# Token rows of the last two experts handed over by 0/1 matrix products, the other rows gathered earlier

## The chip, the cores and the metric

One core of one Trainium2 chip. The time is device microseconds (us) of one execution of the program; what counts is the median over runs.

## What is computed

One step of a one-layer decoder on 512 prompt tokens and 8 x 4 sample tokens (544 rows of 1024 values). After the mixer half (mLSTM memory, causal pooling, projections, layer norm) comes the part that matters here, a mixture of 16 experts with two chosen for each token, and the last layer norm:

```
vals, idx = lax.top_k(jnp.where(in_group, probs, -1.0), TOP_K)      # TOP_K = 2 of 16 experts
wts = vals / jnp.sum(vals, -1, keepdims=True)
gate = jnp.sum(jax.nn.one_hot(idx, N_EXPERTS) * wts[..., None], axis=1)
h = silu(einsum('nd,edf->nef', xt, w_e_gate)) * einsum('nd,edf->nef', xt, w_e_up)
h = h * gate[..., None]
moe = einsum('nef,efd->nd', h, w_e_down)
x = _layer_norm(ALPHA * x + moe, ln2_g, ln2_b)
```

## The kernel before

Every engine has its own program, written by hand in five functions (`_(sp)`, `_(pl)`, `_(ac)`, `_(ve_)`, `_(pe)`), and waits on semaphores by count. There is no scheduler: each engine runs its list in order, so what stands behind a waiting instruction waits too.

Tokens are held in `NT` = 5 row tiles (four of 128 rows and one of 32). For each expert up to `CAP` = 96 tokens have a slot. POOL gathers their rows from the DRAM copy `x1_rows` (`gather`, L739), PE transposes them (`rows_in`, L2146), `up` (L2159) makes gate and up products in PSUM banks 2 and 3, ACT and DVE make the hidden rows (`gate_sigmoid` L1055, `silu` L1643), `hidden_in` (L2179) and ACT (L1051) turn them, and `down` (L2173) makes the 96 result rows in PSUM banks 4 and 5. ACT and DVE copy them to `ys` (L1059; L1649, L1651), and POOL stores them in the DRAM array `y_slots` (`store_y`, L745). The weights of the experts alternate between two sets of buffers that SP fills. One `turn` on PE is: up(e), rows_in(e+1), down(e-1), hidden_in(e).

After the last turn only `down` of expert 15 is left; it waits until ACT and DVE have copied expert 14's result out of the same banks (L2233, L2234). Expert 15's rows are stored by SP in two halves (L664, L666).

The tail gives the tokens their two expert rows. `gather_rows(0, ...)` (L784) fetches, for each row tile, the row of each token's lower-numbered expert (`ya`); it waits for the store of expert 14. `gather_rows(1, ...)` fetches the row of the other expert (`ybk`); it waits for the two halves of expert 15 (`last_out`). Then for each tile: DVE x1 = ya * gate + x1 (L1715); PE adds x1 by an identity (`sum_start`, L2267) and ybk by a diagonal of gates (`sum_end`, L2274) into PSUM; DVE takes the statistics (`stats`, L1723 to L1726) and centres (`centred`, L1730); POOL makes the inverse root (L798); ACT scales (L1113); POOL adds the tile to the output in DRAM (L808), where SP has put the bias before. SP waits for all of them at the end.

Each engine also carries a block `if extra > 0` for experts with more than 96 tokens: it loads a number from `ctl` and branches. It stands between the turns and the tail, and is not entered with these inputs.

## Time and profile before

| | |
|---|---|
| median of 3 runs | 899.44 us (898.88 to 900.25) |
| the profiled execution | 900.57 us, its span 899.3 us |
| PE busy | 867.6 us, 96% of the span |
| DVE, ACT, POOL busy | 360.5, 206.3, 85.6 us |
| mean granted TensorE clock | 0.990 of full speed |
| share of PE in the chain that ended last | 91% |
| idle time of PE before the tail's first product | 5.35 us |
| span after the last product of expert 15 | 37.5 us |

The span runs from the first to the last instruction. PE is busy nearly everywhere except in the last 40 us, where the work is a chain over DMA, PE and DVE.

### The profile page before, as it was taken

Reading aid. Unit: us, or ns where it says so; the run is one execution under the profiler, and the core shown is the slowest. Engines: PE = TensorE matmul, PEld = TensorE weight load, DVE = VectorE, ACT = ScalarE, POOL = GpSimd, SP = SyncE. Lnnn points to the kernel's source line nnn. Section 1 sums busy time; section 2 is a strip of 40 time slices with the busy share of each in tenths; the row PEclk is TensorE's granted clock in tenths of the full one; section 3 lists DMA queues with packets and bytes.
Section 4 is the critical chain, followed back from the end, with each engine's and each line's share of the span. In section 5 each row is a group of like instructions: output and inputs, shape, how many; then the busy total and the mean of one; then the engine's idle time right before and its main releaser. Section 6 shows DMA issues by size and latency. Waiting matters only on the chain.

```text
span 899.3 us, 20975 instructions
## 1 busy us (share of the span) xinstructions
PE 867.6 (96%) x9437; PEld 710.4 (79%) x9437; DVE 360.5 (40%) x749; ACT 206.3 (23%) x313; POOL 85.6 (10%) x89
## 2 busy tenths in 40 slices
PE   7999999999999999999999999999999999999964
PEld 6999888898989999999999988666666566565631
DVE  5653645736575372233232555722311211111146
ACT  4521141311422332322221201231111111111112
POOL 1210000000000001001101021400001000100053
PEclk9999999999999999999999999999999999999987
DMA  9895171492816043222221923699999999999566
GB/s 323 268 286 152 48 264 65 146 313 64 280 48 211 1 156 93 84 67 87 94 95 47 378 102 151 243 371 400 401 404 405 398 410 411 406 404 424 215 210 125
DMA packets 85374, 203.47 MB, mean 226 GB/s; under 512 B 4237, under 2 KB 57189, under 8 KB 76472
## 3 DMA queue, kind: packets, MB, share of 16 engines
q1 hardware_dynamic: 78216, 177.17, 53.5%
q0 software_dynamic: 7088, 25.26, 9.1%
q8 instruction: 57, 0.93, 0.4%
q14 instruction: 13, 0.11, 0.0%
HBM read 172.58 MB, written 32.06 MB: 228 GB/s over the span
## 4 chain that ended last, share of the span: by engine, by line
PE 91%; DMA 4%; DVE 2%; ACT 1%; issue 1%; POOL 0%; SPq 0%; DVEq 0%; POOLq 0%
PE psum L2159 18%; PE psum L465 17%; PE psum L467 17%; PE psum L466 16%; PE psum L2173 9%; PE psum L1863 2%; DMA xg<-x_rows,idx_i 2%; PE psum L1873 2%; PE psum L2146 2%; PE psum L1902 1%; PE psum L2105 1%; PE psum L2072 1%; DMA ya_rows<-y_slots,dest_i 1%; DMA xn<-in_x_prompt_dram 1%; PE psum L1888 1%; PE psum L2037 1%
## 5 line engine op out<-in xcount | busy, mean ns | idle before, releaser
L465 PE MATMUL psum<-x_hi,split_lo 128*128 128x272 f32 x704 | 208.9, 297 | 2.0 <-DVE pbl L1427 1.2
L467 PE MATMUL psum<-x_hi,split_hi 128*128 128x272 f32 x704 | 202.3, 287 | 0.0
L466 PE MATMUL psum<-x_lo,split_hi 128*128 128x272 f32 x704 | 202.1, 287 | 0.0
L2159 PE MATMUL psum<-set,xt 128*32 128x256 f32 x3072 | 169.1, 380 | 0.0
L2159 PEld LDWEIGHTS psum<-set,xt 128*32 128x32 f32 x3072 | 98.2, 110 | 65.7 <-issue 2.4
L465 PEld LDWEIGHTS psum<-x_hi,split_lo 128*128 128x128 f32 x704 | 132.6, 188 | 7.3 <-issue 2.7
L466 PEld LDWEIGHTS psum<-x_lo,split_hi 128*128 128x128 f32 x704 | 132.8, 189 | 1.4 <-issue 1.0
L467 PEld LDWEIGHTS psum<-x_hi,split_hi 128*128 128x128 f32 x704 | 132.6, 188 | 0.0
L460 DVE TENSOR_TENSOR split_lo<-raw,split_hi 128x2048 fp32r<-128x2048 f32 x35 | 80.0, 2290 | 113.8 <-ACT split_hi L441 113.3
L2173 PE MATMUL psum<-set,hT 128*32 128x256 f32 x1536 | 86.2, 380 | 1.5 <-DVE ys L1651 1.5
L2173 PEld LDWEIGHTS psum<-set,hT 128*32 128x32 f32 x1536 | 49.0, 110 | 32.8 <-ACT hT L1051 1.7
L1643 DVE TENSOR_TENSOR gs<-psum,gs 128x384 f32<-128x384 f32 x16 | 8.9, 558 | 152.8 <-ACT gs L1055 152.8
L441 ACT CAST split_hi<-raw 128x2048 fp32r<-128x2048 f32 x35 | 66.7, 1907 | 1.3 <-DMA raw<-in_w_in_dram 1.2
L465 PE MATMUL psum<-split_hi,x_lo 128*128 128x256 f32 x160 | 46.6, 291 | 0.0
L467 PE MATMUL psum<-split_hi,x_hi 128*128 128x256 f32 x160 | 45.1, 282 | 0.0
L466 PE MATMUL psum<-split_lo,x_hi 128*128 128x256 f32 x160 | 44.9, 281 | 0.0
L1055 ACT ACTIVATE gs<-psum 128x384 f32<-128x384 f32 x16 | 7.9, 491 | 156.9 <-PE psum L2159 156.9
L467 PE MATMUL psum<-gh,split_hi 128*128 128x272 f32 x128 | 37.0, 289 | 0.0
L1649 DVE COPY ys<-psum 96x256 f32<-96x256 f32 x16 | 6.7, 421 | 75.4 <-PE psum L2173 75.4
L465 PE MATMUL psum<-gh,split_lo 128*128 128x272 f32 x128 | 36.8, 288 | 0.0
L466 PE MATMUL psum<-gl,split_hi 128*128 128x272 f32 x128 | 36.8, 287 | 0.0
L739 POOL DMA_INDIRECT xg<-x_rows,idx_i x16 | 22.9, 1433 | 143.9 <-PE psum L2146 129.3
(355 smaller groups left out, 1250.3 us busy)
## 6 DMA issues: line engine op xcount, KB each, us to landing
set<-in_w_e_gate_dram SPq DMA_DIRECT2D x32, 1024.0 KB, 18.3
set<-in_w_e_up_dram SPq DMA_DIRECT2D x32, 1024.0 KB, 20.9
set<-in_w_e_down_dram SPq DMA_DIRECT2D x32, 1024.0 KB, 21.2
raw<-in_w_in_dram SPq DMA_DIRECT2D x26, 1024.0 KB, 6.5
cb<-in_state_C_dram SPq DMA_DIRECT2D x8, 1024.0 KB, 7.9
out_dram<-cb SPq DMA_DIRECT2D x8, 1024.0 KB, 5.8
y_slots<-ys POOLq DMA_DIRECT2D x15, 384.0 KB, 7.3
y_slots<-x_hi POOLq DMA_DIRECT2D x3, 1536.0 KB, 14.8
```

The costliest lines, as they stand in the source:

```text
L441: nc.scalar.copy(split_hi[:, c % SPLIT_SLOTS, :], raw[:, c % RAW_SLOTS, :]).then_inc(w_hi, 1)
L460: nc.vector.tensor_tensor(split_lo[:, slot, :], raw[:, c % RAW_SLOTS, :], split_hi[:, slot, :].bitcast(F32), ALU.subtract).then_inc(w_lo, 1)
L465: nc.tensor.matmul(out, a_lo, b_hi, start=first, stop=False)
L466: nc.tensor.matmul(out, a_hi, b_lo, start=False, stop=False)
L467: return nc.tensor.matmul(out, a_hi, b_hi, start=False, stop=last)
L739: pl.indirect_dma_start(xg[e % 2][0:CAP], None, x1_rows, idx).then_inc(g_in[e % 2], 16)
L1863: last = mm(narrow(j)[:, 0:SEQ - i * P], kt[:, c, i * P:i * P + P], qt[:, c, i * P:SEQ], start=c == 0, stop=c == 1)
L1873: last = mm(narrow(j)[:, 0:VW], pb[:, at:at + P], ve[:, i, :], start=i == 0, stop=i == t)
L1888: last = mm(narrow(j)[g * NS:(g + 1) * NS, 0:VW], qm[:, c, 2 * g + b, :], cb[:, 2 * g + b, c, :], start=False, stop=q == 3)
L2146: last = nc.tensor.transpose(out[:, k // 4, k % 4], cols[:, k, :], ident[0:CAP, 0:CAP])
L2159: last = mm(gate_up()[32 * b:32 * b + 32, j], xt[:, kk, 32 * mine:32 * mine + 32], w, start=kk == 0 and j != 1, stop=kk == KT - 1 and j > 0)
L2173: last = mm(results()[32 * b:32 * b + 32, 256 * j:256 * j + 256], h_, w, start=kk == 0 and j != 1, stop=kk == QB and j > 0)
```

## The change

- **Order of the last experts.** PE does the first half of down(14), then turns the hidden rows of expert 15, then the second half, then down(15), whose result goes to PSUM banks 6 and 7 (`results_last`) and whose hidden rows go to an own buffer (`hT_last`), so it no longer waits for the copies of expert 14's result.
- **Rows of experts 14 and 15 stay on chip.** They aren't stored. SP writes zeros over their slots in `y_slots` early in the program (four DMAs of 192 KB), where POOL wrote one of 384 KB before. ACT and DVE multiply each of the 96 rows by its token's gate and split the product in two (`high_part`, `low_part`). Two 0/1 matrices, made by DVE once after turn 4 (`late_slots`), say which slot belongs to which token; PE multiplies them with both parts, straight into the sum (`add_late`).
- **The gates by slot** come from ten more small matrix products in `rows_of(5)` and five more DVE steps in `choice_gates`.
- **Gathers** now wait for the store of expert 13 (and, for the second ones, for up(14)).
- **The second expert's rows** are scaled by ACT (`scaled_second`) and added by POOL (`add_second`) for the four large tiles, in place of PE's diagonal products; for the small tile DVE does it.
- **The block for overfull experts** stands behind the tail on every engine (and makes the output anew if it is entered).

```diff
@@ SP
+                for e in (NE - 2, NE - 1):
+                    for c in (0, 512):
+                        sp.dma_start(y_slots[e * CAP:(e + 1) * CAP, c:c + 512], const("head_sel")[32:32 + CAP, 0:512]
+                                     ).then_inc(zero_out, 16)
...
-        sp.wait_ge(ya_ok, NE)
-        sp.dma_start(y_slots[(NE - 1) * CAP:NE * CAP, 0:512], ys[1][0:CAP, 0:512]).then_inc(last_out, 16)
-        sp.wait_ge(yd_ok, NE)
-        sp.dma_start(y_slots[(NE - 1) * CAP:NE * CAP, 512:DM], ys[1][0:CAP, 512:DM]).then_inc(last_out, 16)
+        sp.wait_ge(outs, 16 * NT)
+        sp.wait_ge(cp_out, 16 * H)
         sp.wait_ge(xa_ok, 1)
         extra = sp.value_load(ctl[0:1, XTRA:XTRA + 1], min_val=0, max_val=XTRA)
@@ POOL
-        for e in range(NE - 4, NE - 1):
+        for e in range(NE - 4, NE - 2):
             store_y(e)
...
-        pl.wait_ge(ys_out[0], 16 * NE // 2)
+        pl.wait_ge(ys_out[0], 16 * (NE // 2 - 1))
         pl.wait_ge(ys_out[1], 16 * (NE // 2 - 1))
-        pl.wait_ge(dn_done, 2 * NE - 2)
         for i in range(NT):
             gather_rows(0, ya, i)
-        pl.wait_ge(last_out, 32)
+        pl.wait_ge(gu_done, 2 * NE - 2)
         for i in range(NT):
             gather_rows(1, yb_, i)
+        def add_second(i):
+            pl.wait_ge(xa2_ok, i + 1)
+            pl.wait_ge(act_rows, SCALED[i])
+            nc.gpsimd.tensor_tensor(x1[:, i, :], x1[:, i, :], yb_[i], ALU.add).then_inc(dg_ok, 1)
+        for i in range(PT):
+            add_second(i)
@@ ACT
+        def high_part(q, b):
+            at = slice(512 * b, 512 * b + 512)
+            ac.wait_ge(ya_ok, NE - 1 + q)
+            if b:
+                ac.wait_ge(yd_ok, NE - 1 + q)
+            nc.scalar.activation(late_y[q][0][0:CAP, at], ys[q][0:CAP, at], ACT.Copy, scale=gslot[0:CAP, q:q + 1]
+                                 ).then_inc(act_rows, 1)
+        def scaled_second(i):
+            ac.wait_ge(yb_in[i], 16)
+            nc.scalar.activation(yb_[i], yb_[i], ACT.Copy, scale=gates_ab[:, 1, i:i + 1]).then_inc(act_rows, 1)
+        gate_sigmoid(2 * NE)
+        ac.wait_ge(hi_done, NE)
+        nc.scalar.copy(hT_last[:], psum[:, 6, 0:QB * P].rearrange("p (q t) -> p q t", q=QB)).then_inc(ht_ok, 1)
+        ac.wait_ge(ys_out[0], 16 * (NE // 2 - 1))
+        store_half(0, 2 * NE - 2)
+        for b in range(2):
+            high_part(0, b)
+        for i in range(2):
+            scaled_second(i)
+        ac.wait_ge(ys_out[1], 16 * (NE // 2 - 1))
+        ac.wait_ge(dn_done, 2 * NE)
+        nc.scalar.copy(ys[1][0:CAP, 0:512], psum[0:CAP, 6, :]).then_inc(ya_ok, 1)
+        for b in range(2):
+            high_part(1, b)
+        for i in range(2, PT):
+            scaled_second(i)
@@ DVE
+        def low_part(q, b):
+            at = slice(512 * b, 512 * b + 512)
+            ve_.wait_ge(yd_ok, NE - 1 + q)
+            ve_.wait_ge(act_rows, HIGH[q][b])
+            v.scalar_tensor_tensor(late_y[q][1][0:CAP, at], ys[q][0:CAP, at], gslot[0:CAP, q:q + 1],
+                                   late_y[q][0][0:CAP, at].bitcast(F32), ALU.mult, ALU.subtract).then_inc(lo_y, 1)
@@ PE
+            if g == len(OH_FIRST) - 2:
+                for q in range(2):
+                    for i in range(NT):
+                        at = 96 * (3 + q)
+                        last = mm(psum[0:CAP, 7, at:at + 96].rearrange("p (a q) -> p a q", a=32), onehot[:, i, NE - 2 + q, :],
+                                  gate3[:, i, q, :].unsqueeze(1).to_broadcast([P, 32, 3]), start=i == 0, stop=i == NT - 1)
...
+        down(0, 8 * NE, 0)
+        pe.wait_ge(hs_ok, NE)
+        hidden_in()
+        down(0, 8 * NE, 1)
         pe.wait_ge(ht_ok, NE)
-        pe.wait_ge(yd_ok, NE - 1)
-        pe.wait_ge(ya_ok, NE - 1)
         for half in range(2):
-            down(1, 8 * NE, half)
+            down(1, 8 * NE, half, hT_last, results_last)
+        def own_rows(i, first=True):
+            r = ROWS[i]
+            pe.wait_ge(xa2_ok, i + 1 if i < PT else NT + 1)
+            pe.wait_ge(dg_ok, min(i + 1, PT))
+            if i >= PT:
+                pe.wait_ge(pf_ok, i - PT + 1)
+            for b in range(2):
+                mm(summed(i)[0:r, b, :], ident[0:r, 0:r], x1[0:r, i, b * 512:b * 512 + 512], start=first, stop=False)
+        def add_late(i, q, first=False):
+            r = ROWS[i]
+            pe.wait_ge(act_rows, HIGH[q][1])
+            pe.wait_ge(lo_y, 2 * q + 2)
+            for part in (1, 0):
+                for b in range(2):
+                    last = mm(summed(i)[0:r, b, :], late[q][0:CAP, P * i:P * i + r],
+                              late_y[q][part][0:CAP, b * 512:b * 512 + 512], start=first and part == 1, stop=q == 1 and part == 0)
+            if q:
+                last.then_inc(pc_ok, 1)
```

How the instructions stand, in two places. On PE, from down(14) on, before (`set_133` and `set_134` are the two weight sets, `x_130` is x1):

```order
L2173 MATMUL psum<-set_133,hT 32x256 x48
L2179 MATMUL psum<-cst,hs 128x128 x3
L2173 MATMUL psum<-set_134,hT 32x256 x48
...
L2267 MATMUL psum<-x_130,cst 128x512 x6
L2274 MATMUL psum<-ybk,diag 128x512 x2
L2267 MATMUL psum<-x_130,cst 128x512 x2
L2274 MATMUL psum<-ybk,diag 128x512 x6
```

and now, up to the end of the second tile (`oh_160` and `oh_194` are the 0/1 matrices of experts 14 and 15):

```order
L2306 MATMUL psum<-set_133,hT 32x256 x24
L2312 MATMUL psum<-cst,hs 128x128 x3
L2306 MATMUL psum<-set_133,hT 32x256 x24
L2306 MATMUL psum<-set_134,hT_last 32x256 x48
L2393 MATMUL psum<-y_lo,oh_160 128x512 x2
L2393 MATMUL psum<-y_hi,oh_160 128x512 x2
...
L2385 MATMUL psum<-x_130,cst 128x512 x2
L2393 MATMUL psum<-y_lo,oh_194 128x512 x2
L2393 MATMUL psum<-y_hi,oh_194 128x512 x2
```

The turning of expert 15's hidden rows moved into the middle of down(14), and each tile's pair of diagonal products gave way to eight with the 0/1 matrices, those of expert 14 ahead of the first two tiles' own rows. On DVE, between the last `silu` and the first statistics, now:

```order
L1713 TENSOR_TENSOR hs<-psum,gs 128x384
L1774 SCALAR_TENSOR_TENSOR x_130<-ya_rows,gates_ab,x_130 128x1024 x2
L1718 COPY ys_172<-psum 96x256
L1720 COPY ys_172<-psum 32x256 x3
L1774 SCALAR_TENSOR_TENSOR x_130<-ya_rows,gates_ab,x_130 128x1024
L1781 SCALAR_TENSOR_TENSOR y_lo<-ys_172,gslot,y_hi 96x512 x2
L1774 SCALAR_TENSOR_TENSOR x_130<-ya_rows,gates_ab,x_130 128x1024
L1795 COPY ys_173<-psum 96x256
L1797 COPY ys_173<-psum 32x256 x3
L1781 SCALAR_TENSOR_TENSOR y_lo<-ys_173,gslot,y_hi 96x512 x2
L1774 SCALAR_TENSOR_TENSOR x_130<-ya_last,gates_ab,x_130 32x1024
L1804 SCALAR_TENSOR_TENSOR x_130<-ybk,gates_ab,x_130 32x1024
```

where before the four copies of expert 14 and the four of expert 15 were followed by the five additions of ya. The first two additions now stand ahead of the copy of expert 14's result.

## Rows read from the trace of the kernel before

**Rows 1.** Chain of waits of the last 100 us: start us, us, what

```profile
838.33 0.48 PE psum L2179 x3
...
849.31 5.22 PE psum L2173 x96
...
863.41 8.18 DMA ya_rows<-y_slots,dest_i
```

**Rows 2.** Timeline of the tail: start us, us, engine, line, instruction [idle before <-releaser]

```profile
856.47 5.39 PE L2173 MATMUL psum<-set,hT 128*32 128x256 f32 x96 [1.50 <-DVE ys L1651]
...
860.82 1.03 POOL L784 DMA_INDIRECT ya_rows<-y_slots,dest_i  x1 [3.19 <-DMA y_slots<-ys]
862.15 0.95 POOL L784 DMA_INDIRECT ya_rows<-y_slots,dest_i  x1 [0.30 <-issue]
862.22 0.42 DVE L1649 COPY ys<-psum 96x256 f32<-96x256 f32 x1 [5.85 <-PE psum L2173]
862.65 1.31 DVE L1651 COPY ys<-psum 32x256 f32<-32x256 f32 x3
...
865.77 1.28 DVE L1715 SCALAR_TENSOR_TENSOR x<-ya_rows,gates_ab,x 128x1024 f32<-128x1024 f32 x1 [1.81 <-DMA ya_rows<-y_slots,dest_i]
...
867.20 7.81 PE L2267 MATMUL psum<-x,cst 128*128 128x512 f32 x12 [5.35 <-issue]
...
876.84 1.30 DVE L1723 BATCH_NORM_STATS2 lst<-psum 128x6 f32<-128x512 f32 x2 [1.45 <-PE psum L2274]
...
885.86 1.28 DVE L1723 BATCH_NORM_STATS2 lst<-psum 128x6 f32<-128x512 f32 x2
...
888.68 1.27 DVE L1723 BATCH_NORM_STATS2 lst<-psum 32x6 f32<-32x512 f32 x2
```

**Rows 3.** Granted clock by stretch: us, POOL busy, clock, DMA share, GB/s

```profile
864.00:865.00 1.00, 0.70 (x2) 0.80 0.85 320
...
871.00:872.00 1.00, 0.90 (x1) 0.79 0.66 111
```

**Rows 4.** The store of expert 13: timeline row, and its issue (KB each, us to landing)

```profile
840.70 0.51 POOL L745 DMA_DIRECT2D y_slots<-ys  x1 [16.82 <-DVE ys L1651]
...
y_slots<-ys POOLq DMA_DIRECT2D x1, 384.0 KB, 5.6
```

**Rows 5.** Timeline, PE: split-type products of 272 columns; full products of 512 columns

```profile
199.83 0.19 PEld L465 LDWEIGHTS psum<-x_hi,split_lo 128*128 128x128 f32 x1
...
200.81 0.19 PEld L467 LDWEIGHTS psum<-x_hi,split_hi 128*128 128x128 f32 x1
...
878.28 5.31 PE L2274 MATMUL psum<-ybk,diag 128*128 128x512 f32 x12
```

**Rows 6.** By line on POOL: duration ns min/median/max, first and last start

```profile
L724 POOL TENSOR_TENSOR sg<-sg,yb x8: 1360/1360/2195, 353.3 to 482.9; 128x544 f32<-128x544 f32 x8
...
L728 POOL TENSOR_TENSOR hrs<-hve,cst x5: 1509/1517/1527, 517.2 to 555.4; 128x1 f32<-128x1 f32 x4, 32x1 f32<-32x1 f32 x1
...
L798 POOL TENSOR_TENSOR hrs<-hve,cst x5: 549/555/563, 878.7 to 890.5; 128x1 f32<-128x1 f32 x4, 32x1 f32<-32x1 f32 x1
```

**Rows 7.** Timeline of two places where DVE and POOL meet

```profile
352.01 2.29 DVE L460 TENSOR_TENSOR split_lo<-raw,split_hi 128x2048 fp32r<-128x2048 f32 x1 [7.81 <-ACT split_hi L441]
...
353.33 2.19 POOL L724 TENSOR_TENSOR sg<-sg,yb 128x544 f32<-128x544 f32 x1 [85.08 <-ACT yb L999]
...
572.94 7.45 DVE L1572 TENSOR_TENSOR onehot<-cst,tmp_r 128x288 bf16<-128x288 f32 x20
...
573.29 7.93 POOL L739 DMA_INDIRECT xg<-x_rows,idx_i  x1 [1.22 <-DVE idx_i L1587]
```

**Rows 8.** Timeline, PE: the 15 small products of one `rows_of`

```profile
646.98 0.82 PEld L2130 LDWEIGHTS psum<-tok_bf,onehot 128*96 128x96 bf16 x15
```

**Rows 9.** Timeline of SP behind its branch

```profile
865.47 0.93 SPq L679 DMA_DIRECT2D out_dram<-nrows  x2
```

**Rows 10.** Timeline of DVE: the silu of expert 5, where the matrices come before it

```profile
676.36 0.56 DVE L1643 TENSOR_TENSOR gs<-psum,gs 128x384 f32<-128x384 f32 x1 [9.69 <-ACT gs L1055]
```

More of the change, by code:

```diff
@@ L297, in build @@
     yb_ = [ybk[:, i, :] for i in range(NT)]
+    hT_last = place("hT_last", [P, QB, P], F32, r_ht + NT * DM * 4)
+    oh15 = place("oh15", [P, N], F32R, at_route + DM * 4)
+    late = (oh14, oh15)
+    y14_hi, y14_lo = lay(r_ht + (NT * DM + QB * P) * 4, r_ht + 4 * CHUNK * 4,
+                         ("y14_hi", [P, DM], F32R), ("y14_lo", [P, DM], F32R))
+    y15_hi, y15_lo = lay(r_moe, end, ("y15_hi", [P, DM], F32R), ("y15_lo", [P, DM], F32R))
+    late_y = ((y14_hi, y14_lo), (y15_hi, y15_lo))
     psum = ctx.enter_context(nc.psum_tensor("psum", [P, 8, 512], F32))
@@ L1655, in _, with late_slots @@
         choice_gates()
+        def late_slots():
+            found = psum[0:CAP, 7, 3 * 96:5 * 96].rearrange("p (e c) -> p e c", c=96)[:, :, 0:3]
+            step(v.tensor_reduce(gslot[0:CAP], found, AX.X, ALU.add))
+            step(v.tensor_copy(tok_f[0:CAP], idx_i[0:CAP, NE - 2:NE]))
+            for i in range(NT):
+                last = v.tensor_scalar(tok_at[0:CAP, :, i:i + 1].rearrange("p e o -> p (e o)"), tok_f[0:CAP],
+                                       float(1 - P * i), None, ALU.add)
+            step(last)
+            for q, oh in enumerate(late):
+                for i in range(NT):
+                    r = ROWS[i]
+                    last = v.tensor_scalar(oh[0:CAP, P * i:P * i + r], const("slot", CAP)[:, 0:r], tok_at[0:CAP, q, i:i + 1],
+                                           None, ALU.is_equal)
+            step(last)
         def turn(e, odd, y_used=None):
@@ L1672, in _ @@
         turn(4, False, y_used=(ys_out[1], 16))
+        ve_.wait_ge(idx_ok, 6)
+        late_slots()
         with ve_.Fori(2, NE // 2 - 1) as t:
@@ new lines, in low_part @@
+        def low_part(q, b):
[4 more added lines that the diff above has]
+                                   late_y[q][0][0:CAP, at].bitcast(F32), ALU.mult, ALU.subtract).then_inc(lo_y, 1)
+        silu(NE - 1)
+        for i in range(2):
+            add_first(i)
+        ve_.wait_ge(ys_out[0], 16 * (NE // 2 - 1))
@@ new lines, in _ @@
+        store_half(0, 2 * NE - 2)
+        add_first(2)
+        low_part(0, 0)
+        low_part(0, 1)
+        add_first(3)
+        ve_.wait_ge(ys_out[1], 16 * (NE // 2 - 1))
+        ve_.wait_ge(dn_done, 2 * NE)
+        v.tensor_copy(ys[1][0:CAP, 512:768], psum[0:CAP, 7, 0:256])
+        for b in range(QB):
+            last = v.tensor_copy(ys[1][b * 32:b * 32 + 32, 768:DM], results_last()[CAP:P, 256 * b:256 * b + 256])
+        last.then_inc(yd_ok, 1)
+        low_part(1, 0)
+        low_part(1, 1)
@@ L1681, in _, with centred @@
+        def centred(i):
+            r = ROWS[i]
+            v.scalar_tensor_tensor(x1[0:r, i, :], summed(i)[0:r].rearrange("p b n -> p (b n)"), hmv[0:r, i, 0:1],
+                                   lng[0:r, :], ALU.subtract, ALU.mult).then_inc(pf_ok, 1)
+        stats(0)
+        for i in range(NT):
+            centred(i)
+            if i < NT - 1:
+                stats(i + 1)
         extra = ve_.value_load(ctl[0:1, XTRA:XTRA + 1], min_val=0, max_val=XTRA)
@@ L2161, in up, with down @@
             last.then_inc(gu_done, 1)
-        def down(p, loaded, half):
+        def down(p, loaded, half, hT=hT, results=results):
             pe.wait_ge(set_in[p][4 + half], loaded)
```

206 lines of the change are left out of this document (114 added, 92 removed).

## The prediction, made before the changed kernel ran

> **What bounds the kernel now.** I read the page first: PE is busy 96% of the span, so up to the last expert only PE's own work counts. Then the chain of waits of the last 100 us, which stays on PE up to down(14), from 849.31 to 854.53 [rows 1], and then leaves it. The timeline shows the rest: down(15) from 856.47 to 861.83 [rows 2]; the store of expert 14, after which POOL may issue the first gather at 860.82; the gathers of ya, of which one took 8.18 us from issue to landing [rows 1]; PE idle for 5.35 us until its first identity product at 867.20 [rows 2]; and from 876.84 on DVE, whose tiles follow each other every 888.68 - 885.86 = 2.82 us, up to the fifth at 888.68 [rows 2]. From there to the end of the span is 899.3 - 888.68 = 10.62 us (statistics, scaling, the last addition to DRAM). The change touches this tail of some 45 us, and elsewhere almost nothing. The reader should see one thing: DVE's statistics start 15 us after down(15) has ended, and those 15 us are what can be won.
>
> **The working, in the times of the trace before.**
>
> *Last down.* With the turning of expert 15's hidden rows (0.48 us [rows 1]) inside down(14), which alone ends at 854.53, PE is through with both by 855.0, and down(15) follows at once: 855.0 + 5.36 = 860.4 instead of 861.83, 1.4 us sooner.
>
> *Gathers.* The store of expert 13 is issued at 840.70 and lands after 5.6 us [rows 4], at 846.3. The first gather then starts at 846.6, after the same 0.27 us as now, 14.2 us sooner than 860.82. Each costs POOL 0.95 us and a gap of 0.30 [rows 2], ten of them 12.5 us, to 859.1. Landing takes between 4.95 us (ya of tile 0: 860.82 to the addition at 865.77 [rows 2]) and 8.18 [rows 1]; I take 5, because the weights, the two stores of SP and the store of expert 14 no longer run beside them. So ya is in DVE's hands from 851.6 on, and the last ybk lands near 864.
>
> *DVE's queue.* Behind silu(15): two additions of ya (1.28 us each [rows 2]), the copies of expert 14 (0.42 + 1.31 [rows 2], from 855.1), one addition, two low parts, one addition, which ends at 860.9; the copies of expert 15 to 862.65; two low parts, the addition and the product of the small tile. A low part of 96x512 isn't in the trace; between the 0.42 us of a copy of 256 columns and the 1.28 us of 1024 columns [rows 2] I take 0.72. With nothing in its way DVE is ready for statistics at 866.7.
>
> *POOL's additions* are new: four of 128x1024. The nearest row is 1.36 us for 544 columns [rows 6]; without a fixed part that gives 2.56 us, with the 0.55 us of the tiny ones [rows 6] as fixed part 2.07. I take 2.4. The GPSIMD Engine Reference of the Trainium skill, Performance versus the Vector engine, has 4.497 us for 2048 columns, of which half would be 2.25; the sum would move by under a microsecond.
>
> *PE's sums.* An identity pair (full precision) costs what the diagonal one did: four records at 0.43, 1.72 us a tile (12 records in 5.31 [rows 5]). A 0/1 product takes the split type. 272 columns follow each other every (200.81 - 199.83) / 8 = 0.1225 us [rows 5]; 512 columns cost 0.22 by columns. Its dearer bound is the full-precision product, 0.86. I take 0.22, as type and shape of the nearer row are the same. A tile from the third on costs 1.72 + 8 x 0.22 = 3.5 us, more than DVE's 2.82, so PE becomes the slower of the two there by 0.7 us a tile.
>
> *Who shares with whom.* This decides the sum. An addition on POOL beside a DVE instruction with both tensors in SBUF took 2.19 us instead of 1.36: it started at 353.33 and DVE ended at 354.30 [rows 7]. A gather issued beside 7.45 us of such DVE work took 7.93 us [rows 7]. The inverse roots of line 728, which meet line 1516 (x1 and ln gain, both SBUF), took 1.52 us; those of line 798, which meet line 1730 (PSUM and gain), 0.55 [rows 6]. So POOL stands still until DVE is done. Whether DVE stands still for POOL no row shows: no DVE row is stretched. By the SBUF page of the Trainium skill, SBUF: two separate sides, the pair of ports is an exclusive lock and "the other fully blocks", either way. The rows on POOL's side agree with it; a gain from an addition that runs free of DVE would need it not to hold.
>
> With blocking: POOL's gathers end near 860.5. The first addition waits for DVE's fourth (860.9) and runs to 863.3, and DVE's low part, due at 862.7, waits for it. Then DVE's four instructions, all ready, run without a gap (2 x 0.72 + 2 x 1.28 = 4.0 us) to 867.3, as the twenty in rows 7 did, and POOL's three remaining additions follow: 869.7, 872.1, 874.5. PE: own rows and both experts of tile 1 end at 872.3, tile 2 at 875.8, tile 3 at 879.3, tile 4 at 882.8. DVE waits for each. The fifth statistics start at 882.9 instead of 888.68; the span would end at 893.5.
>
> *The clock.* PE then pauses from 866.0 to 869.7. Before, the granted clock went to 0.5 between 864 and 865, about 2.8 us into the pause that began at 861.83, and came back after 871, 4.2 us after PE resumed [rows 3]. A pause of 3.7 us may do the same; 4.2 us at half speed cost 2.1 us. I count half, 1.0.
>
> *Small terms.* Ten more small products in `rows_of(5)`: 15 take 0.82 us, so 10 x 0.055 = +0.55 on PE, in full, since PE is the bound there [rows 8]. The 17 DVE steps of `late_slots` fit in the 9.69 us DVE idles before the silu of expert 5 [rows 10], even at its 0.56 us each (9.5); without this cover what exceeds would delay PE's hidden rows. The five steps in `choice_gates` have a similar gap and cost nothing. The zeroing on SP (four issues, 0.77 MB) goes among weight loads three buffers ahead: nothing; uncovered, under 2 us. The overflow block now runs on SP behind the last landing: SP issued the next DMA at 865.47 [rows 9], at most 1.5 us after DVE's copies had let it go on (862.65 + 1.31 [rows 2]), with the issue of a store inside that. Between 0 and 1.5 I take +0.8. On the other engines it hides behind the 6 us in which the last output lands.
>
> Sum: 893.5 + 1.0 + 0.55 + 0.8 = 895.85 for the span against 899.3, a gain of 3.45 us. The profiled execution had 900.57 us, so 897.1 for such a one; against the median of 899.44, **896.0 us**. What a measurement can tell from no change is about 0.2%, 1.8 us.
>
> **The rivals.**
>
> *Turns alternate.* If POOL gets in between any two DVE instructions, each POOL addition delays one of DVE's four. DVE then ends at about 862.7 + 4.0 + 3.3 x 2.4 = 874.6, its tiles follow at 2.82 us, the fifth at 885.9, the span ends at 896.5, and 897.9 with the small terms: 1.4 us less, **898.0 us**. For it: the block as a rule applies both ways. Against: rows 7, where POOL got in only at the end of DVE's run. 25%.
>
> *No blocking.* Additions run beside DVE: statistics from 866.8, PE's 3.5 us tiles end at 878.4, the span at 889.1, 890.4 with the small terms, 8.9 us less: **890.5 us**. Against: rows 6 and 7. It stays possible in part, if the meetings fall elsewhere. 20%.
>
> *Slower: the clock stays low.* PE has 32 split products and five identity pairs after 863, 7.1 + 8.6 = 15.7 us at full clock. If the broken pattern (wait for POOL, 1.7 to 3.5 us of work, wait) keeps the clock at half, they take 31.4 us at least less what hides in waits: from 863.3 to about 890.4, the span ends at 901.0, 902.4 with the small terms, 3.1 us more: **902.5 us**. It decides if the granted clock is 0.5 beyond 875. For it: before, half clock held from 865 to 871 over a busy PE [rows 3]. Against: it came back during just such work. 11%.
>
> *It doesn't do what it says*: gathers landing so late that nothing is won, within 0.2% of 899.4. With 8.2 us to land, the first two additions hold up expert 14's copies by 2 us and little is left of the gain. 4%.
>
> **How the numbers follow.** The forecast has 40%, the rivals 25, 20, 11 and 4. The range 889.6 to 899.9 reaches from below the free case over the alternating one with 2 us of late landing; it leaves out the low clock and some edges. Faster by over 0.2% (below 897.6): the forecast but for its edge (36), no blocking (20), a fifth of the alternating case (5): 0.61. Slower: the low clock, 0.11. Within: 0.28.
>
> **What would show it.** Right: the first gather near 847.2; down(15) without idle before it; no PE idle of 5 us; POOL's additions 2.4 us each or longer where they meet DVE's additions and low parts; PE waiting for POOL's additions from the second tile on; 0/1 products 0.22 us apart; one short stretch at clock 0.5 near 870. Wrong: DVE instructions of 1.28 us stretched to over 2 (alternating), POOL's additions finished by 871 (free), PE at 0.5 beyond 875 (low clock), or 0/1 products 0.4 us apart at full clock, which would put some 6 us on PE and bring back the old time.

## The result, and the profile after

The changed kernel takes **902.21 us** (median, 898.18 to 904.56), the kernel before 899.46 us on the same chip (898.32 to 900.79): a ratio of 1.0027, 95% interval 1.0014 to 1.0039, so 2.4 us slower by the ratio. The prediction said 896.0 us, faster by more than 0.2% with a chance of 0.61, and a range up to 899.9. It was wrong in sign and outside its range. The times of the changed kernel also scatter over 6.4 us, those of before over 2.5 in these twelve runs and over 3.5 to 4.9 in the larger sets beside the experiments.

The profiled execution had 901.96 us, its span 900.7 us. Timeline of the tail (start us, us, engine, line, instruction [idle before <-releaser]), against [rows 2]:

```profile
842.50 0.51 POOL L762 DMA_DIRECT2D y_slots<-ys  x1 [16.82 <-DVE ys L1720]
849.38 1.01 POOL L785 DMA_INDIRECT ya_rows<-y_slots,dest_i  x1 [6.38 <-DMA y_slots<-ys]
...
862.63 0.87 POOL L785 DMA_INDIRECT ybk<-y_slots,dest_i  x1 [0.30 <-issue]
...
863.53 9.27 POOL L798 TENSOR_TENSOR x<-x,ybk 128x1024 f32<-128x1024 f32 x4
...
865.99 8.02 DVE L1781 SCALAR_TENSOR_TENSOR y_lo<-ys,gslot,y_hi 96x512 fp32r<-96x512 f32 x2 [1.50 <-ACT y_hi L1140]
...
866.04 2.38 PE L2385 MATMUL psum<-x,cst 128*128 128x512 f32 x4 [1.90 <-POOL x L798]
866.41 2.17 ACT L1145 ACTIVATE ybk<-ybk,gates_ab 128x1024 f32<-128x1024 f32 x2
...
874.16 1.19 PE L2393 MATMUL psum<-y_lo,oh 96*128 96x512 f32 x2 [5.74 <-DVE y_lo L1781]
...
876.55 1.30 DVE L1812 BATCH_NORM_STATS2 lst<-psum 128x6 f32<-128x512 f32 x2
...
883.26 1.29 DVE L1812 BATCH_NORM_STATS2 lst<-psum 128x6 f32<-128x512 f32 x2 [0.66 <-PE psum L2393]
...
886.84 1.29 DVE L1812 BATCH_NORM_STATS2 lst<-psum 128x6 f32<-128x512 f32 x2 [0.66 <-PE psum L2393]
...
890.65 1.28 DVE L1812 BATCH_NORM_STATS2 lst<-psum 32x6 f32<-32x512 f32 x2 [0.89 <-PE psum L2393]
```

The pair of low parts of expert 15 took 8.02 us; the pair of expert 14, with the same shape, took 1.40. DVE was ready at 865.99, just after POOL had begun its second addition (at 865.85), and the pair ended at 874.03, after POOL's fourth (863.53 + 9.27 = 872.80). PE stood for 5.74 us behind it. The chain of waits says the same: here 6.24 us of "issue" are DVE standing in front of an instruction for which every semaphore was there. (That the landing of `ybk` stands ahead of it in the chain means nothing for the low part, which doesn't read these rows; the wait belongs to the product of the small tile behind it.)

```profile
862.63 4.36 DMA ybk<-y_slots,dest_i
866.99 0.03 issue
867.04 6.24 issue
873.28 0.75 DVE y_lo L1781
```

POOL itself was not slowed. By line, its durations (ns, min/median/max, first and last start):

```profile
L798 POOL TENSOR_TENSOR x<-x,ybk x4: 2330/2352/2369, 863.5 to 870.5; 128x1024 f32<-128x1024 f32 x4
```

The clock, against [rows 3] (stretch, us, busy PE, PEld, DVE, ACT, POOL, granted clock, DMA share, GB/s):

```profile
866.00:868.00 2.00, 1.96 (x4) 0.68 (x4) 2.00 (x1) 2.00 (x3) 2.00 (x1) 0.86 0.07 27
868.00:870.00 2.00, 0.42 (x1) 0.00 (x0) 2.00 (x1) 0.58 (x1) 2.00 (x2) 0.50 0.00 0
...
874.00:876.00 2.00, 1.84 (x4) 1.49 (x5) 1.97 (x3) 0.00 (x0) 0.00 (x0) 0.50 0.00 0
876.00:878.00 2.00, 2.00 (x4) 0.86 (x3) 1.94 (x4) 0.00 (x0) 0.00 (x0) 0.58 0.00 0
878.00:880.00 2.00, 2.00 (x8) 1.21 (x7) 1.74 (x4) 0.50 (x1) 0.57 (x1) 1.00 0.00 0
```

It fell to its lower level (1.2 GHz) between 867 and 868, while PE worked again behind a first idle of 1.90 us, so before the long pause; it stayed there through the pause and for the first 3.5 us of work after it. So the statistics start at 876.55, hardly sooner than the 876.84 of before [rows 2], and then follow at PE's pace of 3.57 us a tile instead of DVE's 2.82.

### The profile page after: what moved, and what is told of

Read it like the earlier page. It is cut to its first block, busy times and chain, and to the rows that moved or that the text cites. A ratio compares the mean times of both kernels' runs of the same rounds, so it can differ in the third digit from the quotient of the medians.

```text
span 900.7 us, 21087 instructions
## 1 busy us (share of the span) xinstructions
PE 870.3 (97%) x9467; PEld 714.9 (79%) x9467; DVE 374.8 (42%) x776; ACT 211.8 (24%) x316; POOL 93.4 (10%) x91
## 4 chain that ended last, share of the span: by engine, by line
PE 91%; DMA 3%; issue 2%; POOL 1%; DVE 1%; ACT 1%; DVEq 0%; SPq 0%; POOLq 0%
PE psum L480 17%; PE psum L482 17%; PE psum L481 16%; PE psum L2292 16%; PE psum L2306 8%; PE psum L1990 2%; DMA xg<-x_rows,idx_i 2%; PE psum L2000 2%; PE psum L2279 2%; PE psum L2029 1%; PE psum L2232 1%; PE psum L2199 1%; PE psum L2393 1%; PE psum L2385 1%; PE psum L2015 1%
## 5 line engine op out<-in xcount | busy, mean ns | idle before, releaser
L2306 PE MATMUL psum<-set,hT 128*32 128x256 f32 x1440 | 81.0, 380 | 0.0
L2306 PEld LDWEIGHTS psum<-set,hT 128*32 128x32 f32 x1440 | 45.3, 110 | 29.8 <-issue 0.2
L480 PEld LDWEIGHTS psum<-split_hi,x_lo 128*128 128x128 f32 x160 | 30.2, 189 | 5.3 <-issue 5.3
```

The source lines that it names most:

```text
L480: nc.tensor.matmul(out, a_lo, b_hi, start=first, stop=False)
L2306: last = mm(results()[32 * b:32 * b + 32, 256 * j:256 * j + 256], h_, w, start=kk == 0 and j != 1, stop=kk == QB and j > 0)
```

## The experiments

The theory after the result: POOL's unbroken run of four additions keeps DVE's low part out of SBUF, and PE, the clock and the whole tail follow. The rivals: PE's longer tiles are the bound in any case; the gathers are late; the low clock is the loss; the new order of the last experts doesn't gain.

**One wait: three of the additions behind the low parts.**

```diff
         for i in range(PT):
+            if i == 1:
+                pl.wait_ge(lo_y, 4)
             add_second(i)
```

> The changed kernel with one wait more: POOL does only its first addition when it is ready, the other three wait until DVE has made all four low parts. Theory (POOL's unbroken run of four additions keeps DVE's low part out): the pair of low parts starts near 866 and takes 1.4 us instead of 8.02, PE has no pause of 5.7 us, the granted clock stays at 1.0 after 866, the additions 2 to 4 take their turn after DVE's two products of the small tile (870), and the fifth statistics start near 886 instead of 890.65: some 4.5 us less than the change, about 897.5 us. Rival (the low part is slow for another reason, such as ACT writing its operand or the data): the pair still takes about 8 us and the time stays at 902. Rival (POOL's total of 9.3 us is the bound, whoever goes first): the additions end near 877 and PE's 3.57 us tiles behind them bring the fifth statistics to 890 to 891, no gain.

Measured: 897.20 us (895.11 to 899.24), ratio to before 0.9974 (0.9961 to 0.9988). One added wait takes some 5 us off the change. Timeline:

```profile
865.96 1.41 DVE L1783 SCALAR_TENSOR_TENSOR y_lo<-ys,gslot,y_hi 96x512 fp32r<-96x512 f32 x2 [1.86 <-ACT y_hi L1142]
...
867.45 8.93 POOL L798 TENSOR_TENSOR x<-x,ybk 128x1024 f32<-128x1024 f32 x3 [1.95 <-DVE y_lo L1783]
868.59 3.24 DVE L1806 SCALAR_TENSOR_TENSOR x<-ybk,gates_ab,x 32x1024 f32<-32x1024 f32 x1
...
886.45 1.28 DVE L1814 BATCH_NORM_STATS2 lst<-psum 32x6 f32<-32x512 f32 x2 [0.89 <-PE psum L2395]
```

The pair takes 1.41 us, the fifth statistics come at 886.45 (expected 886). One thing was not expected: DVE's second small product, issued at 868.59, got in after one addition (3.24 us), and POOL's additions, 3.3 us each twice, waited for DVE in turn. The clock still fell, to 0.50 in 872 to 874, after a later pause of PE (2.24 us, for the second addition), where it had been expected to stay at 1.0.

**No POOL additions: DVE adds the second rows.**

```diff
+        def second(i):
+            ve_.wait_ge(xa2_ok, i + 1)
+            ve_.wait_ge(yb_in[i], 16)
+            v.scalar_tensor_tensor(x1[:, i, :], yb_[i], gates_ab[:, 1, i:i + 1], x1[:, i, :], ALU.mult, ALU.add).then_inc(dg_ok, 1)
...
+        second(0)
         low_part(1, 0)
         low_part(1, 1)
+        for i in range(1, PT):
+            second(i)
```

> The changed kernel with the rows of the second expert added by DVE (product and addition in one instruction of 1.28 us, the first tile's before the low parts, the rest behind them) instead of ACT's scaling and POOL's addition. Theory (POOL's additions are what costs): low parts 0.7 us each, no pause of PE over 2 us, no half clock after 866, the statistics of tile 0 start near 875 (DVE's queue is 4 x 1.28 us longer) and follow every 3.57 us at PE's pace or 2.82 at DVE's, since PE is ahead by then; the fifth near 886.5, total 897 to 898.5 us. Rival (PE's tiles of 3.57 us are the bound wherever they start): the fifth statistics at 890 and 901 to 902 us. Rival (the late gathers are the bound): the second tile's rows land after 870 and DVE waits for a DMA in the tail.

Measured: 895.41 us (894.43 to 896.46, seven runs), ratio 0.9954 (0.9937 to 0.9971), with a scatter of 2 us instead of 6.

```profile
865.16 1.41 DVE L1780 SCALAR_TENSOR_TENSOR y_lo<-ys,gslot,y_hi 96x512 fp32r<-96x512 f32 x2
...
872.68 1.29 DVE L1814 BATCH_NORM_STATS2 lst<-psum 128x6 f32<-128x512 f32 x2
...
883.99 1.27 DVE L1814 BATCH_NORM_STATS2 lst<-psum 32x6 f32<-32x512 f32 x2
```

DVE has 5.1 us more to do and the fifth statistics come 6.7 us sooner. They follow every 2.83 us, so PE's tiles of 3.57 us, started early enough, are no bound, and DVE waits for no landing after 863.96; both rivals fall. Two details were missed: the time is 1.6 us below the expected range (the first statistics come at 872.68 instead of 875), and the clock was at half in 866 to 868. The version also takes four scalings off ACT, so it is less clean a test than the added wait.

**One operand moved: what kind of DVE instruction is kept out.**

```diff
+            src = psum[0:CAP, 6, :] if (q, b) == (1, 0) else ys[q][0:CAP, at]
-            v.scalar_tensor_tensor(late_y[q][1][0:CAP, at], ys[q][0:CAP, at], gslot...
+            v.scalar_tensor_tensor(late_y[q][1][0:CAP, at], src, gslot...
```

> The changed kernel with one operand moved: the first low part of expert 15 takes its result rows from PSUM instead of the copy in SBUF; all else is as in the change. Theory (what a POOL addition keeps out is a DVE instruction with two tensors in SBUF): this low part runs at 866 in 0.7 us beside POOL's additions; the second, which still has both in SBUF, waits until POOL has ended near 873, so the total stays within 1 us of the change (902). Rival (POOL keeps out any DVE instruction that touches SBUF, or ACT's write of the high part is what the low part waits for): the first stays stretched to 7 us or starts late.

Measured: 901.48 us (895.70 to 903.12), ratio 1.0013 (0.9996 to 1.0030).

```profile
862.77 9.26 POOL L798 TENSOR_TENSOR x<-x,ybk 128x1024 f32<-128x1024 f32 x4
...
865.22 0.75 DVE L1782 SCALAR_TENSOR_TENSOR y_lo<-psum,gslot,y_hi 96x512 fp32r<-96x512 f32 x1 [1.49 <-ACT y_hi L1140]
...
865.88 6.71 DVE L1782 SCALAR_TENSOR_TENSOR y_lo<-ys,gslot,y_hi 96x512 fp32r<-96x512 f32 x1
```

Two instructions, one behind the other, of the same shape and writing to the same kind of buffer: with one tensor from PSUM 0.75 us in the middle of POOL's run, with both in SBUF 6.71 us, to the run's end. So it is the second SBUF operand that lets POOL hold DVE up; the time of the whole doesn't move, since the second low part still waits. The SBUF page of the Trainium skill ("SBUF — State Buffer", Who interferes with whom) has the same border: a DVE instruction with two SBUF inputs contends, one with a single SBUF input doesn't. The trace agrees.

**PE kept busy in the pause.**

```diff
             own_rows(i, False)
+            if i == 0:
+                for _ in range(26):
+                    mm(psum[:, 4, :], late[0][0:CAP, 0:P], late_y[0][0][0:CAP, 0:512], start=True, stop=True)
             add_late(i, 1)
```

> The changed kernel with 26 additional products of 512 columns (split type, result not used) on PE in the place where it waits for the low parts of expert 15, so that TensorE does not pause. Theory (the pause costs twice, by itself and by the half clock after it): POOL and DVE as in the change; the granted clock stays at 1.0 from 868 to 878, the first two tiles' products go at full clock, 1.5 to 2 us are won: 900.3 us. Rival (the low clock is the main loss): over 4 us won, below 898. Rival (clock without effect, since the first tile hides it): within 0.5 us of the change, 902.

Measured: 901.09 us (897.95 to 904.49), ratio 1.0012 (0.9995 to 1.0029).

```profile
864.87 8.15 DVE L1781 SCALAR_TENSOR_TENSOR y_lo<-ys,gslot,y_hi 96x512 fp32r<-96x512 f32 x2 [1.46 <-ACT y_hi L1140]
...
866.55 8.02 PE L2404 MATMUL psum<-y_hi,oh 96*128 96x512 f32 x26
...
889.14 1.28 DVE L1812 BATCH_NORM_STATS2 lst<-psum 32x6 f32<-32x512 f32 x2 [0.88 <-PE psum L2393]
```

The clock was at 1.00 from 870 on. The filling ran at half clock at first (an earlier pause of 2.14 us had lowered it) and ended at 874.57, 1.6 us after the low parts, and gave part of the gain back. From its end to the fifth statistics are 14.57 us; in the change, from the end of the low parts, 890.65 - 874.03 = 16.62 us. The half clock costs 2.0 us in these two executions. By the ratios about 1.3 us are won, but the two intervals overlap, so the gain of the whole is not clear of noise; a gain of over 4 us, the first rival, is excluded.

**The new order of the last experts alone**, in the kernel before:

```diff
-        turn(NE - 1, True, 8 * NE, 8 * NE, None)
...
+        down(0, 8 * NE, 0)
+        pe.wait_ge(hs_ok, NE)
+        hidden_in()
+        down(0, 8 * NE, 1)
+        pe.wait_ge(ht_ok, NE)
+        for half in range(2):
+            down(1, 8 * NE, half, hT_last, results_last)
```

> The kernel before with the new order of the last experts alone: the first half of down(14), the turning of expert 15's hidden rows, the second half, and down(15) with its own buffer and its result in banks 6 and 7. By the prediction's term: down(15) starts 1.4 us sooner and all behind it with it, 899.2 - 1.4 = 897.8 us. Rival (the gathers of ya are the bound, since they wait for the store of expert 14, whose copies come no sooner): DVE's first addition stays at 865.8, and the time within 0.5 us of the kernel before.

Measured: 899.55 us (898.77 to 903.54), ratio 1.0012 (1.0001 to 1.0024): no gain.

```profile
855.31 5.36 PE L2188 MATMUL psum<-set,hT_last 128*32 128x256 f32 x96
...
857.92 0.51 POOL L751 DMA_DIRECT2D y_slots<-ys  x1 [16.34 <-DVE ys L1662]
...
861.41 1.02 POOL L790 DMA_INDIRECT ya_rows<-y_slots,dest_i  x1 [2.78 <-DMA y_slots<-ys]
...
866.30 1.28 DVE L1730 SCALAR_TENSOR_TENSOR x<-ya_rows,gates_ab,x 128x1024 f32<-128x1024 f32 x1 [3.75 <-DMA ya_rows<-y_slots,dest_i]
```

down(15) starts 1.2 us sooner than in [rows 2], but down(14), with the turning inside it, ends later, so the store of expert 14 leaves at 857.92 instead of 856.92 (0.4 us of it because the whole tail started later in this execution), and the gathers wait for that store. DVE's first addition comes at 866.30, no sooner than before, so the rival holds. In the change the gathers no longer wait for this store and down(14), the turning and down(15) together are 1.6 us shorter on PE (from 12.73 to 11.16 us); what that is worth to the time of the whole there was not tested.

**A semaphore between the additions.**

```diff
+            if i:
+                pl.wait_ge(dg_ok, i)
             nc.gpsimd.tensor_tensor(x1[:, i, :], x1[:, i, :], yb_[i], ALU.add).then_inc(dg_ok, 1)
```

> The changed kernel with one wait more before each of POOL's additions but the first: for the semaphore of its own previous addition, so that the next is not ready at the moment the previous one ends. Theory (DVE is kept out because POOL's next addition is always ready): the gap lets DVE's first low part in at the next boundary, it takes 2.9 us or less instead of 7.3, the pause of PE falls from 5.7 to about 3 us, and the time to about 899.5. Rival (the gap is too short or does not count): the low part still waits for the fourth addition, 902.

Measured: 899.01 us (896.96 to 902.41), ratio to before 0.9997 (0.9985 to 1.0010).

```profile
864.26 3.50 DVE L1783 SCALAR_TENSOR_TENSOR y_lo<-ys,gslot,y_hi 96x512 fp32r<-96x512 f32 x2 [1.50 <-ACT y_hi L1142]
864.33 2.89 POOL L800 TENSOR_TENSOR x<-x,ybk 128x1024 f32<-128x1024 f32 x1 [0.17 <-POOL x L800]
867.39 2.60 POOL L800 TENSOR_TENSOR x<-x,ybk 128x1024 f32<-128x1024 f32 x1 [0.17 <-POOL x L800]
```

PE's pause for the low parts falls to 0.77 us, and a wait that the data don't need wins about 3 us over the change, by the ratios of twelve runs each. How the gap does it, this execution shows only in part: the first low part became ready at 864.26, just inside the gap (864.16 to 864.33), and so met no addition at all; the second got in at the next boundary, as it also did in faster executions without the added wait (below). The times still scatter over 5.5 us.

**The changed kernel again.**

> The changed kernel itself once more, for its scatter (898.2 to 904.6 us in twelve runs). Theory (the time hangs on when DVE's low part comes against POOL's run of additions, and on when the outputs land): the low part is kept out until the last addition has ended, in whatever run, and the pause of PE is 5 to 6 us; what differs between runs is the start of the tail and the landing of the last output. Rival (in the fast ones DVE gets in between two additions): the low part takes 2 to 5 us and the fifth statistics come 2 to 4 us sooner than at 890.65.

> The changed kernel once more, one look. In the profiled execution of 901.96 us DVE's low part waited until the fourth addition had ended (8.02 us for the pair), in that of 899.11 us it got in where POOL's third addition was not ready (4.75 us). Theory (this alone makes the scatter): a time near 899 goes with a pair of under 6 us, a time of 901 or more with one of 7 us or more. Rival: the time goes with the landing of the last output or the start of the tail instead.

The first of them had 899.11 us, the second 898.65:

```profile
862.01 4.70 POOL L798 TENSOR_TENSOR x<-x,ybk 128x1024 f32<-128x1024 f32 x2 [0.36 <-ACT ybk L1145]
...
865.25 4.75 DVE L1781 SCALAR_TENSOR_TENSOR y_lo<-ys,gslot,y_hi 96x512 fp32r<-96x512 f32 x2 [1.38 <-ACT y_hi L1140]
...
866.94 5.28 POOL L798 TENSOR_TENSOR x<-x,ybk 128x1024 f32<-128x1024 f32 x2 [0.24 <-ACT ybk L1145]
```

```profile
861.89 10.23 POOL L798 TENSOR_TENSOR x<-x,ybk 128x1024 f32<-128x1024 f32 x4 [0.41 <-ACT ybk L1145]
...
864.89 5.01 DVE L1781 SCALAR_TENSOR_TENSOR y_lo<-ys,gslot,y_hi 96x512 fp32r<-96x512 f32 x2 [1.18 <-ACT y_hi L1140]
```

In the first, POOL's third addition was not ready (ACT had not yet scaled its tile), and DVE slipped into the gap. In the second there was no such gap, and DVE got in all the same, after which the two engines took turns. Both fast times go with a pair of about 5 us, the time of 901.96 with one of 8.02, and the fifth statistics come at 887.55 and 887.43: the rival of the first expectation holds, DVE does get in between in the faster ones. But it is not this alone, as the theory of the second one had it: in both, the first gather was issued 1.0 us sooner (848.39 and 848.41 against 849.38). The fairest comparison is the execution with one operand in PSUM, whose first gather came at 848.57 and whose second low part was held: its fifth statistics came at 889.80, some 2 us later than in these two.

One thing differs in step with the outcome. In the three executions with a hold (the change, one operand in PSUM, PE kept busy) ACT had scaled tile 2, and POOL's third addition was ready, some 0.65 us before the second ended; in the two fast ones only 0.1 us after that end, and 0.15 us before it. The probes below show that this can't be the whole rule: there every addition was ready long before.

**The sharing by itself**: phases behind the end of the kernel, in which POOL makes a run of additions and DVE comes in at a chosen time (in the first three phases `bn_stats` from PSUM in front of DVE's products is its delay). Cut to its core:

```diff
@@ POOL
+        nc.gpsimd.tensor_tensor(held[:], minus_half[0:1, 0:1], minus_half[0:1, 0:1], ALU.add).then_inc(pr_p, 1)
+        for i in range(adds):
+            nc.gpsimd.tensor_tensor(ya_rows[:, i, :], yb_[0], yb_[1], ALU.add).then_inc(pr_p, 1)
@@ DVE
+            ve_.wait_ge(pr_p, PROBES_DONE[k] + 1)
+            v.bn_stats(lst[:, 0, 0, :], summed(0)[:, 0, :]).then_inc(pr_v, 1)
...
+            v.scalar_tensor_tensor(outs_[i][0:rows, 0:cols], yb_[2][0:rows, 0:cols], gates_ab[0:rows, 0, 0:1], yb_[3][0:rows, 0:cols],
+                                   ALU.mult, ALU.add).then_inc(pr_v, 1)
```

> The changed kernel with a piece behind its end that measures the sharing by itself (its results go into buffers that are no longer read; the time of the whole is of no interest). Five phases, each begun by both engines together. 1: POOL makes four additions of 128x1024 one behind the other, and 0.7 us after its start DVE comes with two products of 96x512, both tensors in SBUF. 2: the same with two products of 32x1024. 3: as 2, but DVE's second product waits for a semaphore of its first. 4: DVE comes first with four products of 128x1024 one behind the other, POOL with three additions. 5: as 4, but each product of DVE waits for a semaphore of the one before. Theory (whoever runs keeps the other out until its ready instructions are through): in 1, 2 and 3 DVE's first product takes 8 to 9 us, POOL's additions 2.3 each; in 4 POOL's first addition takes 5.1 + 2.3 = 7.4 us and DVE's products 1.28 each; in 5 the gap between DVE's products lets POOL in. Rival (it depends on the shape: products of 32 rows get in at the next boundary, those of 96 don't): 1 as above, in 2 and 3 DVE's first product takes about 3 us and POOL's second addition 3.3. Rival (turns always alternate, and the low parts waited for something else): in 1 too DVE's products take 2 to 3 us each.

```profile
898.20 10.12 POOL L862 TENSOR_TENSOR ya_rows<-ybk 128x1024 f32<-128x1024 f32 x4
...
899.08 2.00 DVE L1880 SCALAR_TENSOR_TENSOR y_lo<-ybk,gates_ab 96x512 fp32r<-96x512 f32 x1
901.01 2.82 DVE L1880 SCALAR_TENSOR_TENSOR y_hi<-ybk,gates_ab 96x512 fp32r<-96x512 f32 x1
...
931.54 8.89 POOL L862 TENSOR_TENSOR ya_rows<-ybk 128x1024 f32<-128x1024 f32 x3
931.72 3.24 DVE L1880 SCALAR_TENSOR_TENSOR y_lo<-ybk,gates_ab 128x1024 fp32r<-128x1024 f32 x1 [4.96 <-POOL held L860]
934.88 3.35 DVE L1880 SCALAR_TENSOR_TENSOR y_hi<-ybk,gates_ab 128x1024 fp32r<-128x1024 f32 x1
```

Turns alternated in all five phases, for every shape, with and without semaphores: this was the last rival, and it contradicts both the theory and what the change shows. One case was not made as planned: in the fourth and fifth phase POOL began 0.14 to 0.18 us before DVE, so a run of DVE that is under way when POOL's first addition comes stayed untested. The second probe varied what still differed (more `bn_stats` in front, `ya_rows[:, i, :]` or `yb_[0]` as POOL's first operand, waits, ACT):

> The changed kernel with seven phases behind its end, as in the probe before (results unused, total time of no interest). In each POOL makes four additions of 128x1024 and DVE comes with two products of 96x512. A: DVE comes 0.7 us after the start, in POOL's first addition (control). B: 2.8 us after it, in the second. C: as B, POOL's additions in place. D: as C, with two fulfilled semaphore waits before each. E: as B, with ACT writing 128x1024 all the while. F: as D, with ACT, and the real low parts. G: DVE comes 4.9 us after the start, in the third addition. In the first probe turns alternated, in the change they did not, so one of these differences must decide. Theory 1 (which addition DVE comes in): A alternates, B to F wait until POOL's fourth addition has ended, some 6.5 us. Theory 2 (ACT's traffic): E and F wait, the others alternate. Theory 3 (waits before POOL's additions, or in place): D and F, or C, D and F wait. Theory 4 (it is arbitration by chance): no pattern over the seven.

A, C, D and F alternated; B and E (7.1 us) and G (5.31 us) waited for the fourth addition. That spoke for "in place or not", which the third probe repeated:

> Nine more phases behind the end of the changed kernel, as in the second probe: POOL makes four additions of 128x1024, DVE comes with two products of 96x512. DVE comes 2.8 us after the start (in the second addition), or 4.9 us (in the third, phases 8 and 9). 1 and 3: POOL adds in place on one set of tiles; 2 and 4: into other tiles, as in phase B; 5: in place on x1, exactly the additions of the change; 6: as 5 with the real low parts; 7: as 6 with two fulfilled waits before each addition; 8: as 5, 9: as 1, DVE coming in the third. Theory (in place or not decides, as in the second probe): 2 and 4 wait for the fourth addition (7 us), all others alternate (2 to 3 us), which would leave the block in the change itself unexplained. Rival (who gets in at a boundary is fixed by nothing that these phases vary): the same form goes either way, 1 unlike 3, or 2 unlike 4, or 5 unlike 6.

Its phases 1, 3 and 8 (1 and 3 are the same code; the last line is the third addition of phase 8):

```profile
898.70 9.22 POOL L869 TENSOR_TENSOR ya_rows<-ya_rows,ybk 128x1024 f32<-128x1024 f32 x4
...
901.37 7.10 DVE L1908 SCALAR_TENSOR_TENSOR y_lo<-ybk,gates_ab 96x512 fp32r<-96x512 f32 x1
...
919.76 10.12 POOL L869 TENSOR_TENSOR ya_rows<-ya_rows,ybk 128x1024 f32<-128x1024 f32 x4
...
922.43 2.51 DVE L1908 SCALAR_TENSOR_TENSOR y_lo<-ybk,gates_ab 96x512 fp32r<-96x512 f32 x1
...
976.25 5.30 DVE L1908 SCALAR_TENSOR_TENSOR y_lo<-ybk,gates_ab 96x512 fp32r<-96x512 f32 x1
976.38 2.33 POOL L867 TENSOR_TENSOR x<-x,ybk 128x1024 f32<-128x1024 f32 x1
```

Phase 1 waited 7.10 us, phase 3 took 2.51, and in both DVE came 2.67 us after POOL's start. Phases 2 and 4 to 7 alternated too, 8 and 9 waited. The rival holds: neither the place of the output nor the moment, to a hundredth of a microsecond, decides, and the two phases with ACT went either way. The three phases with waits before the additions all alternated, but the change has such waits too and was held. Over the three probes DVE got in at the next boundary in 6 of 6 phases when it came during POOL's first addition, and in 9 of 12 when it came some 0.4 us into the second. G, 8 and 9, meant for the third addition, came 0.13 us before it began (976.25 against 976.38), still in the second: all 3 missed that boundary and waited for the fourth addition. No phase came in the third. What decides at a boundary stays open.

**A better version**: the second rows added by DVE, and ACT copies the three 32x256 blocks of expert 15's result.

```diff
-        v.tensor_copy(ys[1][0:CAP, 512:768], psum[0:CAP, 7, 0:256])
-        for b in range(QB):
-            last = v.tensor_copy(ys[1][b * 32:b * 32 + 32, 768:DM], results_last()[CAP:P, 256 * b:256 * b + 256])
-        last.then_inc(yd_ok, 1)
+        v.tensor_copy(ys[1][0:CAP, 512:768], psum[0:CAP, 7, 0:256]).then_inc(yd_ok, 1)
+        second(0)
+        second(1)
@@ ACT
+        for b in range(QB):
+            last = nc.scalar.copy(ys[1][b * 32:b * 32 + 32, 768:DM], results_last()[CAP:P, 256 * b:256 * b + 256])
```

> The version with the second rows added by DVE, and two things more: ACT makes the three copies of 32x256 of expert 15's result in place of DVE, and DVE adds two tiles' second rows before the low parts. In that version DVE is busy without a gap from 864 to the end, so what it sheds (1.31 us) should come off the end: 895.4 - 1.3 = 894.1 us. Rival (PE's tiles become the bound, since the low parts, now behind ACT's longer chain, come over 1 us later): within 0.5 us of 895.4.

Measured: 894.10 us (893.05 to 895.08), ratio 0.9941 (0.9928 to 0.9954): 1.3 us less than with the additions on DVE alone, as expected, though the intervals of the two versions overlap, and faster than both kernels, clear of noise. In the profiled executions the fifth statistics came at 882.29 instead of 883.99.

## Why the prediction was wrong, point by point

**The step that failed** is the one that "decides the sum", under *Who shares with whom*: after POOL's first addition "DVE's four instructions, all ready, run without a gap ... as the twenty in rows 7 did, and POOL's three remaining additions follow". POOL was the one with a run in front of it: the gathers kept it until 863.50, its second addition began at 865.85, the low part came at 865.99, and the third and fourth addition, whose rows ACT had scaled by 867.5 and 868.6, were each ready before the one in front had ended. In the profiled execution POOL's run went through, in the two faster ones turns alternated, and in none DVE's four went first. Twenty DVE instructions holding up one gather [rows 7] were read as a rule for additions too; the fourth phase of the first probe shows that a run of ready DVE products need not hold off POOL's next addition (they took turns). The sum gave the block on DVE's side one addition; the case that happened, DVE behind the rest of POOL's run, was no rival at all.

**What it cost.** With the low parts at 864.7, tile 1 was to be summed at 872.3. It was at 879.65, 7.35 us later: PE went on at 874.16 instead of 869.7 (4.5 us, of which 1.25 are the later start of the tail), had the four products of tile 0 still to do, which the forecast had in front of the pause (0.9), and did it all at half clock (2.0, where the sum counted 1.0). From there on the tiles took 3.57 us, as forecast (3.5).

**A term at nothing: ACT's queue.** The forecast had the low parts due as soon as DVE's own copies had ended. They also need the high parts from ACT, and ACT first scaled tile 1's second rows, whose landing it had waited for, then copied expert 15's result. DVE's low part waited 1.50 us for it (`[1.50 <-ACT y_hi L1140]`). Without that it would have been ready at 864.5, during POOL's first addition, where DVE got in at the next boundary in 6 of 6 phases of the probes. No run tests this order in the kernel itself.

**The turns.** The rival "Turns alternate" gave 898.0 us. The executions in which they did had 899.11 and 898.65, and the version with a gap between additions 899.01. The mechanism was right for these executions: DVE's queue ended at 874.6 and 874.5, where that rival had 874.6. The size is about a microsecond off, because the last two tiles came at PE's pace (3.4 and 3.8 us) and not every 2.82 us. The 25% stood on the wrong case. **"No blocking"** is excluded by the 6.71 against 0.75 us. **"The clock stays low"** gave 902.5, near the measured median, and its sign came true: the clock was at 0.50 beyond 875, until 877.7. Its mechanism did not: it priced all 15.7 us of PE's work at half clock, and the clock was back by 878 and had cost 2.0 us. Without these the time would still be 900, by estimate, so that the number fits is luck.

**The last down.** Without idle, as forecast: down(15) followed down(14) at once. In the kernel before, the same reordering is worth nothing (899.55), because there the gathers wait for the store of expert 14.

**The gathers.** Predicted for 846.6, or 847.2 with the small products; issued at 849.38. Of the 2.2 us, 1.25 are the later start: 1.05 of it lie in the first 14 us (the first split product came at 13.23 instead of 12.18; in the other two executions of the changed kernel at 12.73 and 12.48, and at 12.81 in the version of before with the new order, so most of it is scatter). The store of expert 13 took 6.08 us instead of 5.6 [rows 4], and 0.77 us lay between its landing and the issue, for which 0.27 had been taken. The ten gathers, some of them beside DVE's products (1.4 to 1.7 us instead of 0.94), ended at 863.50 and not at 860.5. Landing took 4.4 to 6.4 us, 5.2 in the median (5 predicted).

**The small terms.** The ten products: the distance from the third gather to the store of expert 13 grew from 249.21 to 249.77 us, 0.56 against 0.55. `late_slots`, `choice_gates` and the zeroing do not show. The overflow block behind the tail: from the fifth statistics to the end of the span 10.05 us against 10.62, so it costs nothing that can be seen, where 0.8 was taken. POOL's additions: 2.35 us each, 2.4 predicted. Products with the 0/1 matrices: 1.85 us for eight, 0.23 each (0.22 predicted).

## What to carry to other kernels

Moving work from a busy engine to POOL is not free for DVE: where both tensors of DVE's instruction lie in SBUF, POOL's queue of ready work can stand in front of it, so put the additions of POOL behind DVE's critical instruction by a semaphore, or let DVE read one operand from PSUM (shown here for one instruction, not for a whole kernel). When two engines exclude each other, write down which one's instructions are ready first and price both orders, one of them as a run. Ask of every operand of the critical instruction which engine's queue it comes from. And a reordering gains only if the thing behind it does not wait for what was made later.

## What the runs showed of the hardware

- A DVE product with two tensors in SBUF was held by POOL's additions for up to three of them (8.02 us for a pair that takes 1.40), across two boundaries between additions of which each could have let it in. The SBUF page of the Trainium skill ("SBUF — State Buffer", SBUF: two separate sides) ties the lock to the whole instruction. The traces agree, in that no held product got in inside an addition, and show besides that the next instruction of the same engine may take it again.
- It is not regular: the same code waited 7.10 us and 2.51 us in one execution. Once DVE has got in, the engines take turns, each waiting for one instruction of the other (additions of 3.3 us for 2.35).
- A low part that became ready inside a gap of 0.17 us between two additions ran at once, and the wait that makes the gap took about 3 us off the change. ACT writing 128x1024 beside it made no difference that these phases show: with it DVE was held once and got in once, as without it.
- With one operand in PSUM DVE was not held (0.75 us beside an addition).
- The versions in which POOL's additions can hold DVE scatter more: 6.4, 7.4 and 6.5 us over twelve runs each (the change, one operand in PSUM, PE kept busy), against 2.0 over seven with the additions on DVE. It is a weak sign: the kernel before, without such a meeting, spread over 4.9 us in thirty runs.
